# Adaptive-norm sums spread one instruction at a time, a later silu, and gate rows made once per layer in a two-block network kernel

## What is computed

```python
for l in range(DEPTH):                      # second block, cut
    m_lat = jnp.split((silu_c  @ ada_w[l] + ada_b[l])[:, None, :], N_MOD, axis=-1)
    m_ctx = jnp.split( silu_cc @ ada_w[l] + ada_b[l],              N_MOD, axis=-1)
    def half_ffn(t, m, j):
        h = modulate(rmsnorm(t, norm_g[l, j]), m[3 * j], m[3 * j + 1])
        return t + 0.5 * m[3 * j + 2] * swiglu_2(h, ffn_w_gate[l, j // 2], ...)
    x, ctx = half_ffn(x, m_lat, 0), half_ffn(ctx, m_ctx, 0)
    x = x + m_lat[5] * y_lat                # mixer: Fourier in layer 0, retention in layer 1
    ...
    x = half_ffn(x, m_lat, 2)
return rmsnorm(x, final_g)
```

## Time and profile before

| | |
|---|---|
| median of 3 runs | 3420.22 us (3417.54 to 3425.39) |
| the profiled execution | 3424.44 us |
| its span on the core | 3422.5 us |
| TensorE busy | 3253.3 us, 95% |
| DVE busy / ACT busy / POOL busy | 2015.4 us, 59% / 1298.5 us, 38% / 115.9 us |
| mean granted TensorE clock | 0.978 of full |
| moved by DMA | 469.29 MB, mean 137 GB/s |

### The profile page before, as it was taken

How to read it: one execution, slowest core, us unless ns; L and a number is a source line. 1 busy time by engine, 2 the same in 40 slices (tenths; PEclk the granted TensorE clock), 3 DMA queues, 4 the chain that set the end, 5 groups by cost and what they waited for, 6 DMA issues and landing times.

```text
span 3422.5 us, 46059 instructions
## 1 busy us (share of the span) xinstructions
PE 3253.3 (95%) x19160; PEld 2806.0 (82%) x19160; DVE 2015.4 (59%) x2437; ACT 1298.5 (38%) x1564; POOL 115.9 (3%) x126
## 2 busy tenths in 40 slices
PE   6998999999999898999999989999999999999898
PEld 6988888888988887898787867787878788877797
DVE  5767557777776657677666745644343334444454
ACT  4444244444445244444322233222232123434343
POOL 0001200000000211000000000000000000000000
PEclk9999999999999999999999999999999999999999
DMA  6552021565553021556544521642232222332652
GB/s 251 232 187 80 28 96 62 211 245 225 221 219 106 27 72 62 216 216 240 141 161 145 181 84 50 172 140 101 81 98 93 98 93 74 122 109 88 176 186 99
DMA packets 95242, 469.29 MB, mean 137 GB/s; under 512 B 18085, under 2 KB 21797, under 8 KB 54330
## 3 DMA queue, kind: packets, MB, share of 16 engines
q1 hardware_dynamic: 77952, 451.44, 37.0%
q10 hardware_dynamic: 17082, 14.90, 1.5%
HBM read 465.23 MB, written 1.09 MB: 136 GB/s over the span
## 4 chain that ended last, share of the span: by engine, by line
PE 63%; DVE 24%; ACT 7%; DMA 3%; issue 2%; ACTq 0%; DVEq 0%; POOL 0%; POOLq 0%
PE ps L100 63%; DVE lo L316 9%; DVE prod L456 5%; ACT hi L310 3%; PE ps L514 1%; DMA half00grow<-gc 0%; DMA half02grow<-gc 0%; DMA retgrow<-gc 0%; DMA fourgrow<-gc 0%; DMA silb<-in_c_c 0%; DMA half12grow<-gc 0%; DVE m0restMs L1942 0%; DVE m1restMs L1942 0%; DVE ct L656 0%; DVE xt L656 0%
## 5 line engine op out<-in xcount | busy, mean ns | idle before, releaser
L316 DVE TENSOR_TENSOR lo<-raw,hi 128x2048 fp32r<-128x2048 f32 (+1 forms) x357 | 809.7, 2268 | 688.9 <-ACT hi L310 673.3
L310 ACT ACTIVATE hi<-raw 128x2048 fp32r<-128x2048 f32 (+1 forms) x357 | 676.1, 1894 | 632.7 <-PE ps L100 539.9
L456 DVE SCALAR_TENSOR_TENSOR prod<-raw,silb 128x1024 f32<-128x1024 f32 x288 | 352.9, 1225 | 15.0
L100 PE MATMUL ps<-half00hs,hi 128*128 128x512 f32 x672 | 213.9, 400 | 6.6 <-DVE lo L316 6.5
L100 PE MATMUL ps<-half02hs,hi 128*128 128x512 f32 x672 | 213.9, 400 | 6.4 <-DVE lo L316 6.3
L100 PE MATMUL ps<-half10hs,hi 128*128 128x512 f32 x672 | 211.4, 396 | 0.7 <-DVE lo L316 0.6
L100 PEld LDWEIGHTS ps<-half00hs,hi 128*128 128x128 f32 x672 | 127.7, 191 | 38.3 <-DVE lo L316 8.3
L100 PEld LDWEIGHTS ps<-half02hs,hi 128*128 128x128 f32 x672 | 127.5, 190 | 38.2 <-DVE lo L316 8.1
L100 PEld LDWEIGHTS ps<-half10hs,hi 128*128 128x128 f32 x672 | 126.2, 188 | 31.4 <-DVE lo L316 1.5
L100 PE MATMUL ps<-half00hs,lo 128*128 128x512 f32 x352 | 140.4, 399 | 0.0
L100 PE MATMUL ps<-half02hs,lo 128*128 128x512 f32 x352 | 140.2, 398 | 0.0
(11 more groups left out here) (896 smaller groups left out, 7810.8 us busy)
## 6 DMA issues: line engine op xcount, KB each, us to landing
raw<-in_ffn_w_gate_up SPq DMA_DIRECT2D x88, 1024.0 KB, 9.1
raw<-in_ffn_gu SPq DMA_DIRECT2D x88, 1024.0 KB, 4.9
raw<-in_ffn_w_down SPq DMA_DIRECT2D x85, 1024.0 KB, 5.1
raw<-in_ada_w SPq DMA_DIRECT2D x72, 1024.0 KB, 4.9
raw<-in_w_in_t SPq DMA_DIRECT2D x28, 1024.0 KB, 4.9
raw<-in_ret_w_in SPq DMA_DIRECT2D x24, 1024.0 KB, 4.8
raw<-in_w_out SPq DMA_DIRECT2D x16, 1024.0 KB, 4.8
raw<-in_w_in_n SPq DMA_DIRECT2D x12, 1024.0 KB, 4.9
```

Of the source, the lines that this page charges most:

```text
L100: return p().matmul(o, l, r, start=start, stop=stop, skip_group_check=True)
L310: a().activation(self.high(w), self.raw[self.place(r)][:, 0:width], ACT.Copy).then_inc(*a.mark(self.wac, w))
L316: v().tensor_tensor(self.low(w), self.raw[self.place(r)][:, 0:width], self.high(w).bitcast(F32), ALU.subtract).then_inc(*v.mark(self.wdv, w))
L456: v().scalar_tensor_tensor(out=K.prod, in0=w[:, m, :], scalar=1.0, in1=K.silb[:, n, :], op0=ALU.mult, op1=ALU.mult, accum_out=K.mods[:, l, ...
```

## The change

There are three edits. The sums: `Ada` gets four phases for a tile, each one sum, and the list places them evenly: with `nt == 2` one after every gate/up tile (from tile 4 on in f10) and two after every down tile; with `nt == 4` four after every gate/up tile. The silu: ACT does it in Ada's first phase. The gates: `GateRows` makes all three gates of a layer at once, from three columns on DVE, one transpose on TensorE into bank 6, a copy by ACT to a [48, 128] tile and one DRAM write with pieces of 512 bytes; it stands behind gate/up tiles 0 and 1 of half00 and half10. `Gates` has one phase, the broadcast load, behind tile 2 (half00, half10) or tile 0 (half02, half12).

```diff
@@ Setup.scalar
-        a.wait_ge(*self.c.all)
-        a().activation(K.silb, K.silb, ACT.Silu).then_inc(*a.mark(self.ac, "sil"))
         yield
@@ class Ada
-    phases = 2 * 36 * 2
+    phases = 2 * 36 * 4
-            self.tiles[2 * i] = [(K.A["ada_w_2"][i // 36, i % 36], 2048)]
+            self.tiles[4 * i] = [(K.A["ada_w_2"][i // 36, i % 36], 2048)]
+
+    def scalar(self, a):
+        a.wait_ge(*self.setup.c.all)
+        a().activation(self.K.silb, self.K.silb, ACT.Silu).then_inc(*a.mark(self.ac, "sil"))
+        for _ in range(self.phases):
+            yield
@@ Ada.vector
             for m in range(2):
-                v.wait_ge(*K.landed(self.mine[i]))
                 for n in range(2):
+                    v.wait_ge(*K.landed(self.mine[i]))
...
-                yield
+                    yield
-class Gates(Stage):
+class GateRows(Stage):
     phases = 2
...
     def vector(self, v):
+        K = self.K
         v.wait_ge(*K.ada.dv["mods", self.l])
+        m = K.mods[:, self.l].rearrange("p (j q c) n -> p j q n c", j=3, q=3)[:, :, 2]
+        for j in range(3):
+            v().tensor_scalar(K.gcol[:, j], m[:, j], 1.0 if j == 1 else 0.5, None,
+                              ALU.mult).then_inc(*v.mark(self.dv, "col", j))
+        yield
+        yield
+
+    def tensor(self, p):
+        self.enter(p)
+        yield
+        p.wait_ge(*self.dv["col", 2])
+        p().transpose(self.K.ps[self.bank][0:48, 0:128], self.K.gcol.rearrange("p j n c -> p (j n c)"),
+                      self.K.ident).then_inc(*p.mark(self.pe, "row"))
         yield
     def scalar(self, a):
         K = self.K
+        yield
+        a.wait_ge(*self.pe["row"])
+        a().activation(K.growt[0:48, :], K.ps[self.bank][0:48, 0:128], ACT.Copy).then_inc(*a.mark(self.ac, "row"))
+        a.wait_ge(*self.ac["row"])
+        a().dma_start(self.rows, K.growt[0:48, :]).then_inc(*self.out.mark())
+        yield
+class Gates(Stage):
+    def scalar(self, a):
         self.enter(a)
-        a.wait_ge(*self.dv["gc"])
-        for n in range(self.n):
-            a().dma_start(self.row[n].rearrange("(c p) -> p c", p=P), K.gcol[:, n, :],
-                          allow_slow_non_contiguous=True).then_inc(*self.out.mark())
-        yield
-        a.wait_ge(*self.out.all)
-        a().dma_start(self.gb, ...)
+        a.wait_ge(*self.rows.out.all)
+        row = self.rows.rows.rearrange("a b -> (a b)")[2048 * self.j:2048 * self.j + 1024 * self.n]
+        a().dma_start(self.gb, row.unsqueeze(0).broadcast_to([P, 1024 * self.n]).rearrange(
             "p (n k) -> p n k", n=self.n)).then_inc(*self.back.mark())
         yield
@@ Ffn.tensor, ahead of the down tiles
+            if k == 0 and self.finish.gates:
+                p.wait_ge(*self.finish.gates.rows.ac["row"])
@@ network: ffn
                 if s.nt == 4:
-                    fill(2)
-                elif j % 3 < 2:
+                    fill(4)
+                elif filled[0] or j > 3:
                     fill()
...
-                    if s.nt == 2 and g[0] % 2 == 0:
-                        fill()
-            fill_slot()
+                    if s.nt == 2:
+                        fill(2)
@@ network: half_ffn
-        gates = put(name + "g", Gates(K, name + "g", [norm], latest[0], l, j, nt // 2, 0.5, gb))
-        latest[0] = gates
+        if j == 0:
+            rows_of.append(put(f"grow{l}", GateRows(K, l, norm, 6)))
+        gates = put(name + "g", Gates(K, name + "g", [norm], rows_of[l], j, nt // 2, gb))
-        return norm, [gates] * gates.phases, s
+        return norm, [rows_of[l]] * (0 if j else 2) + [gates], s
@@ network: Fourier and retention
-    for s in (half, half, four, half, half, four, gates, four, gates, four, four, four, four, four):
+    for s in (half, half, four, half, half, four, gates, four, four, four, four, four, four):
...
-        if q < 2:
+        if q < 1:
             run(gates)
```

More of the change, by code:

```diff
@@ L171, in __init__ @@
         self.mods = m.take("mods", 2, 72, 2)
-        self.gcol = m.take("gc", 2, 8)
+        self.gcol = m.take("gcol", 3, 2, 8)
+        self.growt = m.take("grow", 128)
         self.st = m.take("st", 512)
@@ L602, in gpsimd, with __init__ @@
         yield
-class Gates(Stage):
+class GateRows(Stage):
     phases = 2
[L610 to L614, removed]
+    def __init__(self, K, l, after, bank):
+        super().__init__(K, "grow", f"grow{l}", [after])
+        self.l, self.bank = l, bank
+        self.rows = K.nc.dram_tensor(f"grows{l}", (48, 128), F32, kind="Internal").ap()
+        self.out = Loads(K.sem(f"grows{l}"))
     def vector(self, v):
-        K, at = self.K, 8 * (3 * self.j + 2)
-        if self.before:
-            v.wait_ge(*self.before.out.all)
+        K = self.K
         v.wait_ge(*K.ada.dv["mods", self.l])
-        v().tensor_scalar(K.gcol, K.mods[:, self.l, at:at + 8, :].rearrange("p c n -> p n c"), self.half, None,
-                          ALU.mult).then_inc(*v.mark(self.dv, "gc"))
+        m = K.mods[:, self.l].rearrange("p (j q c) n -> p j q n c", j=3, q=3)[:, :, 2]
+        for j in range(3):
+            v().tensor_scalar(K.gcol[:, j], m[:, j], 1.0 if j == 1 else 0.5, None,
+                              ALU.mult).then_inc(*v.mark(self.dv, "col", j))
         yield
+        yield
[5 more added lines that the diff above has]
+                      self.K.ident).then_inc(*p.mark(self.pe, "row"))
         yield
@@ L627, in scalar, with __init__ @@
         K = self.K
-        self.enter(a)
-        a.wait_ge(*self.dv["gc"])
-        for n in range(self.n):
-            a().dma_start(self.row[n].rearrange("(c p) -> p c", p=P), K.gcol[:, n, :],
-                          allow_slow_non_contiguous=True).then_inc(*self.out.mark())
-        yield
-        a.wait_ge(*self.out.all)
-        a().dma_start(self.gb, self.row.rearrange("n k -> (n k)").unsqueeze(0).broadcast_to([P, 1024 * self.n]).rearrange(
+        yield
[5 more added lines that the diff above has]
+class Gates(Stage):
+    def __init__(self, K, who, after, rows, j, n, gb):
+        super().__init__(K, "gate", who, after)
+        self.rows, self.j, self.n, self.gb = rows, j, n, gb
+        self.back = Loads(K.sem(who + "back"))
+    def scalar(self, a):
+        self.enter(a)
+        a.wait_ge(*self.rows.out.all)
+        row = self.rows.rows.rearrange("a b -> (a b)")[2048 * self.j:2048 * self.j + 1024 * self.n]
+        a().dma_start(self.gb, row.unsqueeze(0).broadcast_to([P, 1024 * self.n]).rearrange(
             "p (n k) -> p n k", n=self.n)).then_inc(*self.back.mark())
@@ L2863, in network @@
     A, order, stages = K.A, K.order, K.stages
-    filled, latest = [0], [None]
+    filled, rows_of = [0], []
     def put(name, stage):
@@ L3051, in network @@
     ffn(s, [norm, norm], late=8)
-    fill_to(18)
+    fill_to(36)
     join(s, rows1, norm)
@@ L3056, in network @@
     gb, rot = K.at(49152, "four_gb", 2, 1024), K.at(59392, "four_fin", 2, 512)
-    gates = latest[0] = put("fourgates", Gates(K, "fourg", [half], latest[0], 0, 1, 2, 1.0, gb))
+    gates = put("fourgates", Gates(K, "fourg", [half], rows_of[0], 1, 2, gb))
     four = put("four", Fourier(K, "four", half, 0, both, Gated(gates, both, rot)))
-    for s in (half, half, four, half, half, four, gates, four, gates, four, four, four, four, four):
+    for s in (half, half, four, half, half, four, gates, four, four, four, four, four, four):
         run(s)
@@ L3068, in network @@
     ffn(half, gates)
-    fill_to(36)
+    fill_to(72)
     before = half
@@ L3085, in network @@
     gb, rot = K.at(57344, "retgb", 1, 1024), K.at(63488, "retfin", 2, 512)
-    gates = latest[0] = put("retgates", Gates(K, "retg", [ret], latest[0], 1, 1, 1, 1.0, gb))
+    gates = put("retgates", Gates(K, "retg", [ret], rows_of[1], 1, 1, gb))
     rout = put("retout", Out(K, "retout", [ret], A["ret_w_out_2"][0], yT, ys, Gated(gates, K.xa, rot), 6))
```

10 lines of the change are left out of this document (4 added, 6 removed).

## The result

The median of 4 runs is 3340.26 us (3338.66 to 3342.01), that of the kernel before, run beside it, 3420.31 us. The ratio is 0.9764, 95% interval 0.9752 to 0.9776: 80 us faster.

The account below looks back on a forecast made before the run. TensorE was taken to bound nearly all of the span. Start and sums 42.6 plus gates 40.4 less 0.6 added work made 82.4 us; 3420.2 - 82.4 = 3337.8, stated as 3337, range 3323 to 3360.

Parts of the forecast that it names:

- start and sums: First block, f10 to f21: earlier start plus evenly spread sums in gate/up and down tiles, 42.6 us gained together.
- rival A: First block: sums tiles hold load-ring places, so loads come late; 3377 us (chance 0.04), or landing beyond 11.5 us, slower (0.02).
- Start: f10's third tile starts at 33.4 instead of 43.12, with 2.5 us of wait left; gain 9.7 us.
- Gate/up tiles: f10, f20, f11, f21: every gate/up tile at 5.615 us; gains 6.8, 5.5, 5.5 and 8.4 us.
- the clock term: f10: 1.7 us left for slow clock behind the remaining 2.5 us wait, lowering its gain from 8.5 to 6.8.
- The count of a round: ACT-DVE rounds, first block: two sums lengthen 5.3 us to 6.4; one leaves 5.3, under TensorE's 5.615.
- Down tiles: f10 to f21: two sums fit after each down tile, stretches fall from 273.35 to 266.7 us; gain 6.7.
- half00, half02, half10: Gate-write waits go from all three; half00 and half02 gain 7.8 + 8.1 = 15.9 us, half10's late splits were hidden.
- what was left out: half00 and half02: counted by TensorE's idle time and slow clock, they may give 2.6 us more, not in the sum.
- Fourier and retention: Gate-write waits removed: 7.7 us in the Fourier mixer, 11.3 us at retention's output projection.
- The new write: Gate rows to DRAM: nearer a plain load's 4.9 us, no wait counted; at 16.7 up to 5.5 us a layer.
- Added work: Per layer, small DVE columns, a TensorE transpose, an ACT copy and an issue; loss 0.6 us in the sum.

Follow-up runs that it names:

- the version with both small edits: Changed kernel with DVE's wait for four late constant loads behind f10's third-tile split and half00's first tile split one down tile of f21 later: 3335.43 us.

## Why the prediction was right, point by point

The total came out within 3.3 us, but this is in part luck, since by steps two errors cancel: start and sums gave about 7 us less than predicted, and the three stages with 512 columns about 8 more, by the memory map, which the prediction did not mention (its own run gives 4.6 for the whole, 0.3 to 7.2). Luck too is the kernel before that it was held against: beside another group of runs the same change gained 69.7 us. Of the signs set down, these held: the wait at the start, tiles at 5.60 to 5.65 us, no wait for the landing of a gate write, DVE's idle of 7.70 us in the Fourier mixer gone, a clock of 0.988. Two did not: half00 and half02 took 367.2 instead of 370 to 371, and ACT's splits in f10 to f21 do wait for loads, which was the sign of rival A and of being wrong; the waits are there, but hidden.

**Start.** Predicted 33.4 for the third tile and a wait of 2.5 us, ended by a split held by the late loads; measured 33.21, 2.13, and the run with the wait moved shows its releaser. The 1.7 us for slow clock behind it were not paid: the windows above grant 1.00 from 33.21 on. The 2.39 us at the end of f21 were paid for, with 0.50 granted from 1570.8 to 1574.2, and so were the 2.66 at the same place in the changed kernel run again; the 2.46 in the run with the wait moved and the 2.44 with the sums alone were not. The Trainium skill (TensorE: Matmul & The Clock Gate, on what's actually happening) has the array fall once it has idled. Here waits of nearly one length at one place were followed by a fall in some executions and not in others, so a wait of 2 to 3 us should be priced at anything from nothing to 1.7 (half of 3.4 us).

**Gate/up tiles.** Predicted 6.8 (8.5 without the clock term), 5.5, 5.5, 8.4; measured 7.8, 6.0, 5.2, 8.1. The count of a round (one sum and a subtraction fit beside ACT's split, two don't) holds in all four stages, the norm in f21 included.

**Down tiles.** Predicted a gain of 6.7, measured a loss of 1.1 (273.35 to 274.42). This is the step that failed. "Two sums after each down tile make 2.5 + 2.3 = 4.8 us of DVE in 5.5, where nothing else stands": in f21 the spare tile of half00 stands there too, and its load was held up by the ring. That is 5.2 of the 7.8, as the run with a later spare split shows, 1.7 of them slow clock behind the wait. About 1.2 lie in f10, whose down stretch takes 68.16 here, with 0.6 of idling, and 67.0 in the version with both small edits. The rest is, by its size, the map: half12's own down stretch, my yardstick, went from 66.67 to 67.07, four times 0.4.

**Rival A** was there, in mild form: 44 splits that wait 96 us in all for loads, ACT 2.2 us late in the mean and up to 7.7, nearly all of it hidden but for the end of f21. The count (ACT 1.2 us late, hidden up to 5.6) was a little low for the first and held for the second; with one place less the mechanism decides the kernel, at 1.0179. The lead of the eighth place is worth more than I had counted, and what is left of it is about 3.4 us (5.6 - 2.2, an estimate from the two sums above).

**half00, half02, half10.** Predicted 15.9 (18.5 with what was left out) and measured 26.3 over the three stages. With the map alone the three give 2.4, 2.7 and 1.1, the last with a slow stretch in it. Taking for half10 the whole 3.4 as the map's share, the map gives 8.5 of the 26.3 and the waits 17.8 (376.1 - 367.2 in half00 and in half02, both with the new map), inside my bounds. One such stage moves by 3 us between executions, so the shares are good to a few us: with the old map and the gate writes half00 and half02 took 378.6 and 377.8 (sums alone), 381.2 and 375.1 (silu alone).

**Fourier and retention.** 6.3 for 7.7 and 10.5 for 11.3; half12 5.2 for 5.5. The Fourier figure means little by itself, since the same program differed by 5.5 us there; the mean clock rose with it from 0.89 to 0.92. I had written that the scattered write "also stands in the way of loads, which is one more thing that goes"; no run shows a split that waited for a load on its account. What it did was to land late and, in numbers, to hold the engine that issued it.

**The new write.** I put a plain load's 4.9 us on it; both landed in 2.8 us, and nothing waits. The Trainium skill (DMA: Bandwidth & Descriptors, Specifications) wants at least 512 bytes in a piece for full rate. The trace agrees as far as it goes: 24 KB in pieces of 512 bytes land in 2.8 us, 4 KB in pieces of 4 bytes in 9.7 to 30.1. No run here varies the length of the pieces between the two.

**Added work** cost what was put down or less: half00 has no wait over 0.6 us in its gate/up tiles.

## What to carry to other kernels

Where two engines hand a tile to each other, put fillers in single instructions, one per round, and check the round against the bound engine's time; then look at what the filler holds (here a place of the load ring) and at every out-of-order split that is written for the old pace. Let nobody wait for a small write's landing, and transpose before writing so that the pieces are long: both count, since six scattered writes that nobody waited for still held the engine that issued them for 11 to 12 us. When an edit allocates memory, run the kernel before with that allocation alone, or its effect is booked to the edit.

## What was not expected of the hardware

The time between matmuls depends on where the operands lie. Windows of TensorE over six gate/up tiles of half10 (288 matmuls of 512 columns, no wait, full clock), for the kernel before, for before with the new map, for the changed kernel, and for it with the free area at a multiple of 2048 bytes; for the first two also four down tiles:

```profile
2751.50:2818.70 67.20, 67.20 (x290) 1.00 0.29 94
2835.40:2879.40 44.00, 44.00 (x194) 1.00 0.21 72
```

```profile
2747.30:2813.20 65.90, 65.90 (x290) 1.00 0.27 96
2829.70:2874.50 44.80, 44.80 (x194) 1.00 0.21 71
```

```profile
2681.90:2747.80 65.90, 65.90 (x290) 1.00 0.28 96
```

```profile
2691.00:2757.90 66.90, 66.90 (x289) 1.00 0.27 95
```

A gate/up matmul takes 67.20 / 288 = 233 ns in the old map, 229 in the new one and 232 in the third; a down matmul 44.00 / 192 = 229 in the old and 233 in the new. So one map is good for some operands and bad for others, and a stage of 370 us moves by 3. Other executions agree: over six such tiles it is 67.10 us with the sums alone (old map) and 65.96 in the changed kernel run again (new map). Which distance between which operands decides it was not found.

The other finding is the spread that is no edit's doing: the same kernel before had medians from 3404.8 to 3420.3 us in different groups of runs, on the same chip 3419.6 and 3408.8, and one program's Fourier stretch took 107.4 and 112.9 us in two executions. The first is larger than anything that the two small edits gave, the second larger than the 3.6 us by which they lowered the median.
